# A hybrid decoder step on one core: V units among index units, bisection shared by VectorE and ScalarE, state scan moved beside it

## What is computed

```python
h = rms_norm(x, norm1_g)
u, q, k, v, qi, ki, wi, g_ssm, g_attn = split(h @ w_in)
# branch A: 32 groups of 16 channels, complex diagonal state of 64 per group
h_t = ab * h_{t-1} + bb @ u_t                 # associative scan over positions
y_ssm = glu(gelu(Re(C h_t) + D u_t))
# branch B: indexer and top-k
s = relu(einsum('bthd,bsd->bths', qi, ki) * IDX_DIM ** -0.5)
sc = where(key_pos <= q_pos, einsum('bths,bth->bts', s, wi * N_IDX_HEADS ** -0.5), -inf)
_, idx = top_k(sc, min(256, L // 4))          # 256 of 1024; 129 of 516 for the samples
y_attn = softmax(q k[idx] / 8 + bias) @ v[idx]
x = x + W_o(sigmoid(g_ssm) * (y_ssm @ w_ssm_out) + sigmoid(g_attn) * (y_attn @ w_attn_out))
x = x + relu(rms_norm(x) @ w_up) ** 2 @ w_down
```

## Time and profile before

| what | us |
|---|---|
| time, median of 3 runs | 1986.42 |
| lowest and highest | 1984.13 and 1988.11 |
| the profiled execution | 1991.1 |
| its span in the profile | 1989.3 |
| TensorE busy in it | 1781.6 |
| VectorE, ScalarE, GpSimd busy | 994.8, 560.2, 405.5 |

### The profile page before, as it was taken

The page is one execution under the profiler, slowest core; times in us unless marked ns, Lnnn a source line. Parts: engine busy times, 40 slices in busy tenths (PEclk is TensorE's granted clock), DMA queues, the critical chain, the costliest instruction groups (busy, mean ns, idle before and its releaser), DMA issues. The chain is left out here.

```text
span 1989.3 us, 28408 instructions
## 1 busy us (share of the span) xinstructions
PE 1781.6 (90%) x11112; PEld 1572.0 (79%) x11112; DVE 994.8 (50%) x1941; ACT 560.2 (28%) x1057; POOL 405.5 (20%) x213
## 2 busy tenths in 40 slices
PE   3859567899999999788798996999999999999999
PEld 2849426799998975555598996999999999999887
DVE  3855987999995537553242141333333333333334
ACT  5323260121423225442321133222222222222220
POOL 5208000011121000000543133122111111111110
PEclk9979787899999998998898997999999999999999
DMA  5171107462231105005452212011111111111102
GB/s 143 48 118 44 33 18 59 101 169 90 90 95 60 47 20 172 1 1 155 149 169 86 84 47 64 22 43 43 43 51 54 42 42 42 42 42 42 42 21 87
DMA packets 120468, 135.33 MB, mean 68 GB/s; under 512 B 23490, under 2 KB 101282, under 8 KB 120338
## 3 DMA queue, kind: packets, MB, share of 16 engines
q1 hardware_dynamic: 120370, 134.01, 24.0%
HBM read 109.80 MB, written 24.18 MB: 67 GB/s over the span
## 5 line engine op out<-in xcount | busy, mean ns | idle before, releaser
L2514 DVE TENSOR_TENSOR view_at<-psum,view_at 128x512 f32<-128x512 f32 (+1 forms) x288 | 199.2, 692 | 183.1 <-PE psum L141 183.1
L139 PE MATMUL psum<-mix_hi,up_hi 128*128 128x352 f32 x768 | 250.0, 325 | 13.9 <-DVE hid_lo L2505 10.3
L140 PE MATMUL psum<-mix_lo,up_hi 128*128 128x352 f32 x768 | 248.2, 323 | 0.0
L141 PE MATMUL psum<-mix_hi,up_lo 128*128 128x352 f32 x768 | 247.8, 323 | 0.0
L139 PE MATMUL psum<-dn_hi,hid_hi 128*128 128x512 f32 x576 | 227.6, 395 | 0.0
L141 PE MATMUL psum<-dn_hi,hid_lo 128*128 128x512 f32 x576 | 226.7, 394 | 0.0
L2505 DVE TENSOR_TENSOR hid_lo<-psum,hid_hi 128x352 fp32r<-128x352 f32 x96 | 50.4, 525 | 352.3 <-ACT hid_hi L2471 352.3
L140 PE MATMUL psum<-dn_lo,hid_hi 128*128 128x512 f32 x576 | 226.3, 393 | 0.0
L1419 DVE TENSOR_SCALAR_CACHE_REDUCE view_at<-view_at,view_at 128x384 bf16<-128x384 f32 (+6 forms) x231 | 196.0, 912 | 1.2
L139 PE MATMUL psum<-h_hi,w_hi 128*128 128x352 f32 x600 | 194.8, 325 | 0.1
L140 PE MATMUL psum<-h_lo,w_hi 128*128 128x352 f32 x600 | 193.1, 322 | 0.0
(11 more groups left out here) (351 smaller groups left out, 3456.3 us busy)
## 6 DMA issues: line engine op xcount, KB each, us to landing
view_at<-w_in SPq DMA_DIRECT2D x18, 1024.0 KB, 5.4
view_at<-w_up SPq DMA_DIRECT2D x16, 1024.0 KB, 5.7
view_at<-w_down SPq DMA_DIRECT2D x16, 1024.0 KB, 4.8
gate_dram<-view_at SPq DMA_DIRECT2D x48, 176.0 KB, 1.9
view_at<-gate_dram SPq DMA_DIRECT2D x16, 528.0 KB, 4.4
view_at<-cache_k SPq DMA_DIRECT2D x32, 256.0 KB, 3.1
view_at<-cache_v SPq DMA_DIRECT2D x32, 256.0 KB
view_at<-u_dram SPq DMA_DIRECT2D x16, 290.0 KB, 15.3
```

What stands on the lines that cost most here:

```text
L139: nc.tensor.matmul(out, lhs[0], rhs[0], start=start, stop=False)
L140: nc.tensor.matmul(out, lhs[0], rhs[1], start=False, stop=False)
L141: return nc.tensor.matmul(out, lhs[1], rhs[0], start=False, stop=stop)
L2514: nc.vector.tensor_tensor(x1[r, i, cols], psum[r, 4 + (2 * par + j) % 4, :], x1[r, i, cols], ALU.add).then_inc(add_done, 1)
```

## The change

**Stage 1.** norm1's gains alone stay on SyncE's queue, behind two tiles of x, with their own semaphore; the other 13 parameters are issued by GpSimd, behind its first small operations and ahead of its h_lo. VectorE's gains wait for norm1's gains only. The bias has four store buffers. The 8 loads of Uc ahead of the kernel store are gone. One constant is new, hideb, the identity times -HIDE.

**Stage 2.** The 12 sets, the initial states, the turn table and the scan have left. An index unit has one of 3 slots; the two banks that this sets free take V units of the first column half, nine of them, each behind one of the pairs that hold units 5, 9, ... 37, evacuated by ScalarE and stored by SyncE. Pages are loaded as soon as the index weights' load is issued. The 8 loads of Uc are issued once the last index unit is computed.

**Stage 3.** TensorE's order is: 12 sets and two transposes of initial states, 9 V units, 48 gate units, Y sets, transposes of the final states, 36 QK units, 12 GLU units. ScalarE copies both halves of the sets and, from the fourth round of the bisection on, counts tiles 3, 6 and 7 (512, 896 and 1024 keys) as sums of Sign(threshold - score), between V and gate evacuations at places given by rounds_by_v and rounds_by_gate (two rounds for three gates). VectorE counts the other four tiles, as complements (is_lt), with three small operations a round, and does the scan's 8 plain scans of 128x128 at rounds 13, 15, 18 and 20. GpSimd does the rotations before and behind them. After 32 rounds come a count of all tiles, a nudge of the threshold by one unit in the last place, a count of ScalarE's tiles, and four mask operations a tile in place; masks hold 0 or 1 as complements and TensorE multiplies them by hideb. M and the u blocks (Uy) are loaded behind gate store 35. The weights of the next chunk are loaded ahead of the store of the fifth gate of six. The GELU runs behind QK unit 18's root. VectorE no longer waits for the gate stores ahead of GLU.

The diff, cut to its core:

```diff
-            for i in range(4):
+            for i in range(2):
                 load_x(i)
-            sp.dma_start(par_in[0:GP, 0, :], ...).then_inc(par_loaded, 16)
...
+                sp.dma_start(g1c[:, :], a["norm1_g"]...).then_inc(g1_in, 16)
+            for i in range(2, 4):
+                load_x(i)
...
+            pool.dma_start(par_in[0:GP, 0, :], ...).then_inc(par_loaded, 16)
...
                 if i == 1:
-                    dve.wait_ge(par_loaded, 16 * 14)
+                    dve.wait_ge(g1_in, 16)
...
-            for t in range(L):
-                sp.dma_start(Uc[GI * t:GI * (t + 1), :, :],
-                             u_dram.rearrange("(g i) t c -> t i g c", i=GI)[L - 1 - t]).then_inc(uc_in, 16)
             sp.wait_ge(kern_ev, 9)
...
-                if u >= 4:
-                    pe.wait_ge(relu_done, u - 2)
+                if u >= 2:
+                    pe.wait_ge(relu_done, u - 1)
...
+                if u + 1 in FILL:
+                    n = FILL.index(u + 1)
...
+                    for k in range(KD):
+                        last = split_mm(psum[:, 6 + n % 2, 0:WC], h_parts(k, tok0(n), tok0(n) + P), w_parts(5, k, 0, WC),
+                                        k == 0, k == KD - 1)
+                    last.then_inc(v_mm, 1)
...
+            for n, (c, m, t3) in enumerate(GJ):
+                if n % 6 == 4:
+                    sp.wait_ge(mm_done, G0 + n + 2)
+                    load_w(sp, 9 + c)
+                sp.wait_ge(out_done, G0 + n + 1)
+                sp.dma_start(gate_dram[2 * c + m, :, TH * t3:TH * (t3 + 1)], gst[:, n % 2, :]).then_inc(g_st[n % 2], 16)
+                if n == 35:
+                    sp.wait_ge(m_zero, 1)
+                    for t in range(L):
...
+            def count_until(r_end):
+                while counted[0] < r_end:
+                    act.wait_ge(thr_done, counted[0] + 1)
+                    for i in ACT_TILES:
+                        j = i - FIRST
+                        nc.scalar.activation(mask_of(i), scores(i), ACT.Sign, bias=thr_f[:, j:j + 1], scale=-1.0,
+                                             accum_out=cnt[:, j:j + 1]).then_inc(act_counted, 1)
+                    counted[0] += 1
...
+                    link(count(ALU.is_lt, [i for i in tiles if i not in ACT_TILES]))
+                    dve.wait_ge(act_counted, len(ACT_TILES) * (r - ALONE + 1))
+                    link(v.tensor_tensor(keep_b, cnt, allow2, ALU.is_le))
```

More of the change, by code:

```diff
@@ L815, in _ @@
                                      wi_dram.rearrange("(g b t) h -> b h t g", b=BG, t=NS)[b, h]).then_inc(wcol_in, 16)
+            for n in range(NT):
+                sp.wait_ge(v_out, n + 1)
+                sp.dma_start(rows(nv, n)[:, 0:WC], vst1[own(n), n % 2, :]).then_inc(v_st[n % 2], 16)
+            load_w(sp, 7)
+            sp.wait_ge(unit_mm, len(UNITS))
+            sp.wait_ge(qiS_done, 2)
+            for t in range(L):
+                sp.dma_start(Uc[GI * t:GI * (t + 1), :, :],
+                             u_dram.rearrange("(g i) t c -> t i g c", i=GI)[L - 1 - t]).then_inc(uc_in, 16)
@@ L956, in _ @@
             link(v.memset(wsel, 0.0))
-            dve.wait_ge(turned, 1)
-            for q in range(2):
-                scan(v, link, q)
             dve.wait_ge(kw_ev, 2)
@@ L1054, in _ @@
                         half = slice(64 * odd, 64 * odd + 64)
-                        last = mm(psum[:, 2 * ((u + odd) % 4) + n0 // 512, 0:n1 - n0], qiT[half, h // 2, i * P:(i + 1) * P],
+                        last = mm(psum[:, 2 * ((u + odd) % 3) + n0 // 512, 0:n1 - n0], qiT[half, h // 2, i * P:(i + 1) * P],
                                   kiT[half, n0:n1], start=True, stop=True)
@@ L1131, in hybrid_kernel @@
     need = small(NTK)
+    allow = small(NTK)
+    allow2 = small(NTK)
+    nudge = small(NTK)
+    ONE_ULP = 2.0 ** -24 * (1 + 2.0 ** -12)
+    ACT_TILES = (3, 6, 7)
+    ALONE = 3
     H4 = WC // HD
@@ L1250, in _, with link @@
         def _(pool):
+            tt = nc.gpsimd.tensor_tensor
+            chain = [0]
+            def link(ins):
+                chain[0] += 1
+                ins.then_inc(pool_chain, 1)
+                pool.wait_ge(pool_chain, chain[0])
+            link(pool.memset(S[:, :, :, 0:1], 0.0))
+            split_low(pool, 7)
+            pool.wait_ge(out_done, I0 + 1)
+            start = [S[:, r, :, NC + 1:NC + 1 + NB] for r in range(2)]
+            late = [S[:, r, :, NC + 2 + NB:SC] for r in range(2)]
@@ new lines, in _ @@
+            a4 = [aps4[:, r, :].unsqueeze(2).broadcast_to([P, GP, NB]) for r in range(2)]
+            t1, t2 = (x[:, 0:GP * NB].rearrange("p (g b) -> p g b", b=NB) for x in turn_t)
+            for r, (x, y, op) in enumerate(((start[0], start[1], ALU.subtract), (start[1], start[0], ALU.add))):
+                link(tt(t1, a4[0], x, ALU.mult))
+                link(tt(t2, a4[1], y, ALU.mult))
+                link(tt(t1, t1, t2, op))
+                link(tt(ends[:, r].rearrange("p b g -> p g b"), t1, late[r], ALU.add))
@@ new lines, in parts, with into_frame @@
+            def parts(q):
+                pair = slice(4 * q, 4 * q + 4)
+                return [S[:, r, pair, 1:1 + NC] for r in range(2)] + [turn[:, r, pair, :] for r in range(2)] + rot[q % 2]
+            def into_frame(q):
+                sr, si, cr, ci, ta, tb, tc, td = parts(q)
+                link(tt(ta, cr, sr, ALU.mult))
+                link(tt(tb, ci, si, ALU.mult))
+                link(tt(tc, cr, si, ALU.mult))
+                link(tt(td, ci, sr, ALU.mult))
+                link(tt(ta, ta, tb, ALU.add))
+                ins = tt(tc, tc, td, ALU.subtract)
+                link(ins)
+                pool.memset(mark, 0.0).then_inc(rotated, 1)
```

545 lines of the change are left out of this document (275 added, 270 removed).

## The result

| kernel | median us | lowest to highest | runs |
|---|---|---|---|
| before | 1985.28 | 1982.12 to 1988.11 | 4 |
| changed | 1968.09 | 1964.50 to 1969.81 | 4 |

The ratio is 0.9914, with a 95% interval of 0.9899 to 0.993: the change takes 17 us off, 0.9%. The forecast was 38 us off, to 1948; the sign was right, the size was not, though 1968 lies inside 1926 to 1970.

The account below looks back on a forecast made before the run. It looked to TensorE's waits in the first 746 us. Savings of 20 (stage 1), 6.2 (stage 2) and 12.2 (stage 3), 38.4 us in all, took 1991.1 to 1952.7, or 1948 on the median's scale; range 1926 to 1970.

Parts of the forecast that it names:

- Stage 1: First projection stage: earlier gains and a kernel store without loads ahead of it let it end about 20 us earlier.
- rival B: Stage 1: GpSimd issues slowly, 2.1 us each, and the whole stage moves by 14, to 1962 us; chance 0.15.
- Stage 2: Second projection stage: sets and the scan wait leave, V units come in between index units; 6.2 us off, bounds 0 to 12.
- u's loads: End of stage 2: u_dram's 8 loads run beside the 21 us tail; up to 20 us if that cover failed.
- Stage 3, start: Ahead of the gates: sets and 9 V units take 37.0 us instead of 72.3, -35.3, with +2 for the clock.
- gate 44: Gates of stage 3: TensorE stalls about 9 us because gate store 36 stands behind 16 loads; bounds 0 to 15.
- Stage 3, bisection beside the gates: Stage 3's gates: ScalarE and VectorE share the counts at 4.1 us a round, at 0 cost on the path.
- The port's price: Bisection rounds: GpSimd running beside VectorE's small operations can put 1 us on a round now and then.
- the cover: Stage 3's gates: evacuation hides in six banks up to about 5.6 us a round; each us above costs 29.
- the sign of being wrong: Bisection beside the gates: rounds above 5.6 us in the changed kernel's profile would make the forecast wrong.
- Rival C: Bisection: VectorE's three small operations each wait for GpSimd, rounds reach 6.2 us, gates move by 17, to 1965; chance 0.11.
- Stage 3, rest: QK units: state stores add 2.7 us and the moved GELU block 9.4; Y, QK and GLU units keep their time.

Follow-up runs that it names:

- run 11: The changed kernel with the 8 loads of u again ahead of the kernel store at stage 1's end: 1981.0 us.
- run 10: The changed kernel with the 13 parameter transfers back on SyncE's queue, behind norm1's gains and four tiles of x: 1968.35 us.
- run 6: The changed kernel with 16 loads spread over gate stores, three rounds in five gates, high weight part ahead of counts, state stores earlier: 1938.3 us.
- run 7: The changed kernel with 2 of the 8 scans in each of the four scan groups, the other 24 left out: 1953.4 us.
- run 4: The changed kernel with three rounds of the bisection in five gates instead of two in three: 1958.5 us.
- run 1: The changed kernel with GpSimd's rotations left out and four memsets in place of each one's first half: 1947.9 us.
- 9: As run 6, with the GELU block in two halves, behind QK units 18 and 27: 1937.65 us.

## Why the forecast was right and wrong, point by point

**Stage 1: right** (-19.0 for -20). Both steps held: the gains (first gain at 9.57 for 9.2, u matmuls at 52.9 for 52.3) and the store without the loads (3.8 us for 4.9, undone in run 11). The unknown price of an issue on GpSimd, between 5.5 and 58 us for 13, was 9.3, so 0.7 each where rival B needs 2.1; run 10 shows that even this price is hidden. One step in it was wrong: four bias buffers did not remove the 6.15 us wait, it is 5.06. The first bias store, issued at 102.46 behind 1 MB of weights, frees its buffer only at 110.1; why so late was not tested. It cost under 1 us, since VectorE's tables end at 112.7 and the kernel matmuls start at 113.5.

**Stage 2: right in mechanism, better in size** (-10.3 for -6.2). Units from 189.0 to 264.7 are 75.7 us for 78. Before, the first units stood ahead of the 20.5 us wait and took 2.1 us (218.35 to 240.99 less the wait); the sum counted them in its 78 and did not take them off the old side. The projections did not grow by the 1 us put down for them. u's loads were not quite hidden, which the forecast named as its risk: 6.1 us of wait at 286.8. In the profiles of all eleven runs stage 3 starts 23.7 to 24.4 us behind the issue of the first of these loads, as here (262.76), so their landing sets the start. The wait itself is 2.7 us in some profiles and 6.2 in others only because TensorE's last work ahead of it runs at one or the other clock. The row of the changed kernel (granted clock 1.00 from 277.7 on), then that of run 6 (0.50):

```profile
278.72 2.01 PE L988 MATMUL psum<-view_at,view_at 128*32 128x512 f32 x8
...
280.24 3.79 PE L988 MATMUL psum<-view_at,view_at 128*32 128x512 f32 x8
```

Both start stage 3 at 286.8. So the loads cost 3.4 us at most, the 6.1 less the 2.7 that a start without a late load takes (run 7).

**Stage 3, start: right.** 37.4 us for 37 + 2; **gate 44: right in mechanism**, 13.6 for 9. The 36.9 us behind the first load agree with the earlier trace rows. What I left out is that the loads go out when ScalarE has evacuated gate 35, not when TensorE has computed it; run 4, with no lag at gate 35, shows 9.6, and run 1 10.2.

**Stage 3, bisection beside the gates: the step that failed.** The forecast put 4.1 us on a round and 0 on the path; the profile has 11.4 us of stops for w_lo, most of the 4.6 by which gate 44 missed, and 5.3 of slower matmuls. Three things were wrong in it. The scans were put at nothing, with no reason given: four groups of eight, 28.0 us, where without a neighbour they are 10.5. The port's price was put at "1 us now and then" on small operations, and it was 47 us for 91 of them instead of 15.5. And the cover was reckoned with the mean round against six banks, while ScalarE's queue also held the high part of the next weights, for which there are two buffers and no banks. What stopped TensorE first was this. Run 1 shows that GpSimd's rotations are behind the lag (22.3 us at gate 18, 5.0 without them), and run 7 that most of it came in the scan groups.

Rounds 3 to 31 took from 304.9 to 493.8, 6.5 us each, above the 5.6 named as the sign of being wrong. One of them is the 13.5 us round with ScalarE's wait for raw weights; behind the last scan group, from 436 on, most take 3.7 us, and VectorE waits for ScalarE again. Rival C, priced at 1965, has the right cause, VectorE waiting for GpSimd. But it names only the small operations, where run 7 puts most of the lag on the scans, and it has each slow round move the gates, where TensorE stood once for a chunk's weights. That 1965 lies near 1968 is therefore partly luck. Its condition, that GpSimd is busy in this stretch, was misjudged: GpSimd is busy 117.0 us of the gates' 213.8, 79 of the first 102. The Trainium skill, "SBUF — State Buffer", section Who interferes with whom, has a tensor_tensor with both inputs in SBUF contend with GpSimd's reads; run 1 agrees (the tensor_tensor of a round goes from 20.5 us in all to 16.2), and shows it for scans, which that sentence does not name: 28.0 down to 15.0.

**Stage 3, rest: right.** QK units 133.4 us for 134.8, the GELU stop 6.9 us for 9.4 and the first units' waits 5.5, where before had 2.9 and the forecast added 2.7. GLU took 33.3 us instead of 30.0, with a clock of 0.91 instead of 1.00 and the same matmuls; it is 30.4 at a clock of 1.00 in runs 4 and 9, so these 3 us come and go between executions.

**Behind:** -2.9 us was not forecast. The same code took 1238.0 to 1242.4 us in the profiles of the other runs, 1240.3 in this one and 1243.2 in the one profile of before, so most of it may be chance. It is not explained.

## What to carry to other kernels

When work is shared between two engines in rounds, each round is a two-way wait, and everything queued behind it on either engine inherits the slower one's longest step. Reckon the lag at the worst round, against the shallowest buffer behind it, not the mean against the deepest. A batch of loads on a queue that also carries paced stores is better let out one or two at a time at the stores' pace (14 us here), and a store that a stage's end waits for is better issued with no loads ahead of it (12 us here). When a stop vanishes and the time stays, look for the next stop of the same lag before calling the edit useless.

## What the runs showed of the hardware

- A scan of 128x128 on VectorE waits for GpSimd's running operation as small two-input operations do: 0.40 us alone, 1.3 to 1.5 beside a rotation that takes 1.2 to 1.3, and 4.8 beside a weight part that takes 4.6. The counts with an accumulator kept their 0.61 to 1.28 us beside both.
- An issue of a transfer by GpSimd took 0.49 to 1.22 us of its time, 9.3 us for 13.
- A Sign with accumulation over 1024 elements took 1.14 us on ScalarE, over 512 it took 0.72. With the reads of the sums, 0.19 each and mostly overlapped, the three take 3.0 us from first start to last end, against 3.1 estimated.
- SyncE took 24.6 us to issue the 16 loads of M and u, 1.5 us each, and a store behind them was not issued before.
- The last 24 matmuls of stage 2 took 3.0 us in four profiles and 4.8 to 5.7 in the others, at a granted clock of 1.00 and 0.50 (its two levels, 2.4 and 1.2 GHz), with the same code in stage 2. Why the clock differs is open.
